# A hybrid encoder block in fp32: value projection with 512 columns for six of eight token tiles, and three re-ordered places

## The reference

```python
u = rmsnorm(h); proj = u @ w_in                  # 1024 x 4096
qa, ka, va, hq, hff, hfb, hi, hg = split(proj, 512 each)
y_na = neighbourhood_attention(qa, ka, va)       # 8 heads of 64, grid 16 x 64, window 8 x 16
y_hg = bidirectional_gated_recurrence(hq, hff, hfb, hi, hg)   # 4 heads of 128, v = hi
h = h + concat(y_na, y_hg) @ w_out
u = rmsnorm(h); h = h + square(relu(u @ w_up)) @ w_down       # hidden 4096
```

## Time and profile before

| | us |
|---|---|
| three runs | 1292.2, 1293.55, 1294.88 |
| median | 1293.55 |
| profiled execution | 1293.81 |
| its span, first to last instruction | 1292.0 |
| PE / weight loads / DVE / ACT / POOL busy | 1274.4 / 1072.9 / 845.6 / 587.4 / 473.9 |

### The profile page before, as it was taken

How to read it: one execution, slowest core, us unless ns; L and a number is a source line. 1 busy time by engine, 2 the same in 40 slices (tenths; PEclk the granted TensorE clock), 3 DMA queues, 4 the chain that set the end, 5 groups by cost and what they waited for, 6 DMA issues and landing times.

```text
span 1292.0 us, 17686 instructions
## 1 busy us (share of the span) xinstructions
PE 1274.4 (99%) x6432; PEld 1072.9 (83%) x6432; DVE 845.6 (65%) x1268; ACT 587.4 (45%) x1058; POOL 473.9 (37%) x259
## 2 busy tenths in 40 slices
PE   7999999999999999999999999999999999999998
PEld 6878888998888889878888788888888888888887
DVE  3537666641869686976486654554555888888885
ACT  6346766445536354350345554454453433433341
POOL 3241212115030503045135544444443544544452
PEclk9999999999999999999999999999999999999999
DMA  7341332222010202152311744544559463533423
GB/s 247 129 131 49 82 103 83 83 66 82 1 50 1 66 1 68 47 185 74 134 49 58 243 139 146 166 137 145 166 203 374 138 238 98 190 133 102 162 86 144
DMA packets 134469, 154.92 MB, mean 120 GB/s; under 512 B 11376, under 2 KB 89584, under 8 KB 134384
## 3 DMA queue, kind: packets, MB, share of 16 engines
q1 hardware_dynamic: 131216, 147.04, 35.7%
q10 hardware_dynamic: 3168, 6.75, 1.4%
HBM read 109.72 MB, written 44.04 MB: 119 GB/s over the span
## 4 chain that ended last, share of the span: by engine, by line
PE 92%; DVE 4%; ACT 1%; issue 1%; DMA 1%; POOL 0%; ACTq 0%; SPq 0%; DVEq 0%
PE bank L2359 8%; PE bank L2362 8%; PE bank L2363 8%; PE bank L2328 7%; PE bank L2331 7%; PE bank L2332 7%; PE bank L2070 6%; PE bank L2066 6%; PE bank L2069 6%; PE bank L2153 4%; PE bank L2289 2%; PE bank L2285 2%; PE bank L2288 2%; PE bank L1964 1%; PE bank L1966 1%
## 5 line engine op out<-in xcount | busy, mean ns | idle before, releaser
L885 POOL TENSOR_TENSOR w_hi<-stage,one_col 128x1024 fp32r<-128x1024 f32 x32 | 61.3, 1917 | 409.6 <-DVE scores L1615 176.4
L943 POOL TENSOR_TENSOR a_split<-a_raw,a_split 128x1024 fp32r<-128x1024 f32 x56 | 148.0, 2663 | 166.1 <-ACT a_split L1223 166.1
L2328 PE MATMUL bank<-set,w_hi 128*128 128x512 f32 x448 | 177.8, 397 | 0.7 <-DVE s L1860 0.6
L2331 PE MATMUL bank<-set,w_hi 128*128 128x512 f32 x448 | 176.1, 393 | 0.0
L2332 PE MATMUL bank<-set,w_lo 128*128 128x512 f32 x448 | 176.0, 393 | 0.0
L2359 PE MATMUL bank<-w_hi,a_split 128*128 128x512 f32 x448 | 174.6, 390 | 0.2
L2363 PE MATMUL bank<-w_hi,a_split 128*128 128x512 f32 x448 | 174.3, 389 | 0.0
L2362 PE MATMUL bank<-w_lo,a_split 128*128 128x512 f32 x448 | 174.3, 389 | 0.0
L2066 PE MATMUL bank<-uT_hi,w_hi 128*128 128x512 f32 x384 | 158.7, 413 | 0.0
L2070 PE MATMUL bank<-uT_hi,w_lo 128*128 128x512 f32 x384 | 150.5, 392 | 0.0
L2069 PE MATMUL bank<-uT_lo,w_hi 128*128 128x512 f32 x384 | 149.7, 390 | 0.0
(11 more groups left out here) (227 smaller groups left out, 2748.9 us busy)
## 6 DMA issues: line engine op xcount, KB each, us to landing
a_raw<-a_dram SPq DMA_DIRECT2D x56, 512.0 KB, 3.8
a_dram<-abuf SPq DMA_DIRECT2D x111, 256.0 KB, 2.1
stage<-in_w_in SPq DMA_DIRECT2D x29, 512.0 KB, 4.1
raw<-in_w_down SPq DMA_DIRECT2D x10, 1024.0 KB, 8.0
stage<-in_w_up SPq DMA_DIRECT2D x16, 512.0 KB, 5.1
raw_b<-in_w_up SPq DMA_DIRECT2D x16, 512.0 KB, 5.7
x_tok<-in_x SPq DMA_DIRECT2D x8, 512.0 KB, 8.5
v_dram<-vs ACTq DMA_DIRECT2D x16, 256.0 KB, 2.3
```

The lines of the kernel that those rows point to most:

```text
L943: pool.tensor_tensor(split_of(m, 1), a_raw[:, m % 4, :, :], split_of(m, 0).bitcast(F32), ALU.subtract).then_inc(b_lo, 1)
L2328: first = pe.matmul(dst, w[0], u[0], start=k == 0 and p in (1, 5, 6, 7), stop=False, skip_group_check=True)
L2331: pe.matmul(dst, w[0], u[1], start=False, stop=False, skip_group_check=True)
```

## The change

1. Value units. Token tiles 0 and 1 keep two units of 256 columns each; token tiles 2 to 7 get one unit of 512 columns, ("hv", 2, t), over all four value tiles. The order is ("hv", 0, 0), ("hv", 0, 1), the six wide units, ("hv", 1, 0), ("hv", 1, 1). A wide unit is cut into two pieces of four feature blocks. The sixteen pieces stand at the places of the sixteen units before. PE gives back two ring slots at the first matmul of ("hv", 1, 0), and two at the first after ("hv", 1, 1).
2. Tile 15 is split without the wait for the bias.
3. Tile 35 is split after `o_sq_rest >= 8` instead of after the last level; SP loads all residual tiles before tile 37.
4. In block 2 of the up products DVE makes `up_results` before the sums of weights of block 3.
5. The first query-key mean stands after four feature blocks of the next unit instead of two.

```diff
-    u += [("hv", c, t) for c in range(2) for t in range(TT)]
+    u += [("hv", 0, t) for t in HALF_TOKENS] + [("hv", 2, t) for t in FULL_TOKENS] + [("hv", 1, t) for t in HALF_TOKENS]
...
-VALUE_UNITS = {9: (0, 1), 10: (2, 3), 11: (4, 5, 6), 12: (7, 8, 9), 13: (10, 11), 14: (12, 13), 15: (14, 15)}
-VALUE_AT = {(s, 2 * i if s == 9 else i): j for s, js in VALUE_UNITS.items() for i, j in enumerate(js)}
+VALUE_PIECES = [(("hv", 0, t), range(KT)) for t in HALF_TOKENS]
+VALUE_PIECES += [(("hv", 2, t), ks) for t in FULL_TOKENS for ks in (range(4), range(4, KT))]
+VALUE_PIECES += [(("hv", 1, t), range(KT)) for t in HALF_TOKENS]
+VALUE_STEPS = {9: (0, 1), 10: (2, 3), 11: (4, 5, 6), 12: (7, 8, 9), 13: (10, 11), 14: (12, 13), 15: (14, 15)}
+VALUE_AT = {(s, 2 * i if s == 9 else i): j for s, js in VALUE_STEPS.items() for i, j in enumerate(js)}
...
-                if n == N_IN + RING + 2:
-
                     sp.wait_ge(o_mean, 2 * HG_HEADS)
                     load_resid(range(3, TT))
...
-                if 10 <= n < 16:
+                if 10 <= n < 15:
                     pool.wait_ge(bias_done, bias_ops(2 * n - 19))
...
+                elif n == N_IN + RING - 1:
+                    pool.wait_ge(o_sq_rest, 2 * HG_HEADS)
...
-                    act.activation(h_v[:, part, 256 * what:256 * what + 256], b[:, 0:256], ACT.Copy).then_inc(act_freed, 1)
+                    c0, w = (0, 512) if what == 2 else (256 * what, 256)
+                    act.activation(h_v[:, part, c0:c0 + w], b[:, 0:w], ACT.Copy).then_inc(act_freed, 1)
...
+                if j == 2:
+                    up_results(j)
                 if j == UPS - 1:
                     down_weights(0)
                 else:
                     for p in (7, 5):
                         up_sum(UP_AT[(j + 1, p)])
-                up_results(j)
+                if j > 2:
+                    up_results(j)
...
-                    done = 2 * (p1 == TT - 1)
+                    done = 2 * ((UNITS[n - 1][1], p1) in ((2, TT - 1), (1, HALF_TOKENS[-1])))
...
-                    tile = TILE_OF[("in", C_HV + 256 * what)]
-                    pe.wait_ge(w_split, 2 * (tile + 2))
+                    c0, tiles = (0, 4) if what == 2 else (256 * what, 2)
+                    tile = TILE_OF[("in", C_HV + c0)]
+                    pe.wait_ge(w_split, 2 * (tile + tiles))
...
-                        w = [t[:, r:r + 2, P * k:P * k + P] for t in ring]
-                        dst = b[:, 0:256]
+                        w = [t[:, r:r + tiles, P * k:P * k + P] for t in ring]
+                        dst = b[:, 0:P * tiles]
...
-                projection(n, range(2))
+                ahead = 4 if n == FIRST_QK + 1 else 2
+                projection(n, range(ahead))
                 qk_average(n - 1)
-                projection(n, range(2, KT))
+                projection(n, range(ahead, KT))
```

More of the change, by code:

```diff
@@ L128 @@
 N_TILES = len(TILES)
+HALF_TOKENS, FULL_TOKENS = (0, 1), tuple(range(2, TT))
 def proj_units():
@@ L995, in unit @@
                 elif kind == "hv":
-                    if what == 0 and part < NG:
+                    if what != 1 and part < NG:
                         act.wait_ge(score_done, NG * (NB * (PAIRS - 1) - 1) + part + 1)
-                    act.activation(h_v[:, part, 256 * what:256 * what + 256], b[:, 0:256], ACT.Copy).then_inc(act_freed, 1)
+                    c0, w = (0, 512) if what == 2 else (256 * what, 256)
+                    act.activation(h_v[:, part, c0:c0 + w], b[:, 0:w], ACT.Copy).then_inc(act_freed, 1)
                 elif kind == "hq":
@@ L1273, in _ @@
                     qk_root(qk)
-                values = [UNIT[("hv", 0, 0)] + i for i in VALUE_UNITS.get(s, ())]
-                for n in values[:1] if s > 9 else ():
+                values = [VALUE_PIECES[j] for j in VALUE_STEPS.get(s, ())]
+                values = [[UNIT[u]] if ks[-1] == KT - 1 else [] for u, ks in values] + 4 * [[]]
+                for n in values[0] if s > 9 else ():
                     unit(n)
@@ L1278, in _ @@
                     take_pT(s, 2)
-                for n in values[1:2] if s > 9 else ():
+                for n in values[1] if s > 9 else ():
                     unit(n)
@@ L1282, in _ @@
                     take_pT(s, 3)
-                for n in values[2:]:
+                for n in values[2]:
                     unit(n)
@@ L1295, in _ @@
                     if s == 9 and g == 1:
-                        unit(values[0])
+                        unit(values[0][0])
                 if s == 9:
-                    unit(values[1])
+                    unit(values[1][0])
                 if s >= 0:
@@ L2223, in share @@
                     if (s, i) in VALUE_AT:
-                        projection(UNIT[("hv", 0, 0)] + VALUE_AT[(s, i)])
+                        u, ks = VALUE_PIECES[VALUE_AT[(s, i)]]
+                        projection(UNIT[u], ks)
                 if s >= 0:
```

## The result

The changed kernel took 1299.57 us in the median of six runs (1298.39 to 1301.24); the kernel before, beside it on the same chip, 1293.04 (1292.2 to 1294.88). The ratio is 1.0046, with a 95% interval of 1.0036 to 1.0057: slower by about 6 us, a small loss but clear of the noise (the medians differ by 6.5). The profiled execution took 1300.29 us with a span of 1298.5, which is 6.5 more than the span of before.

A forecast was written before the change was run, and what follows sets the result against it. TensorE (PE), busy 99% of the span, was taken as the bound; gains of 4.8 us against costs of 10.55 gave net +5.7 on 1293.81, less 0.26: 1299.3 us, range 1295.0 to 1303.0.

The forecast's parts named there:

- the main step: At step 15, later slot return delays tile 16's split, tile 18's load and band 15 behind it; PE waits 8.05 us.
- T: Moment PE starts the first matmul of ("hv", 1, 0), the first piece of step 15; 281.98 in the kernel before.
- Stall: PE's wait for band 15 before step 15's first product with it: 8.05 us, bounds 7.7 and 9.3.
- POOL's part: POOL starts splitting tile 16 at T + 0.51 and has it split at T + 4.9.
- the landing: Time from issue to landing of band 15's last DMA, behind tile 18's load: taken as 2.4 us.
- Clock: PE's clock falls in the wait for band 15 and slows the rest of step 15: 2.0 us lost, bounds 0 and 3.
- rival 2: The wait for band 15 comes but PE's clock stays up: 1297.3 us; chance 15%.
- Step 9: Tile 15's earlier split on POOL meets DVE's two probability multiplies: cost 0.5 us, bounds 0 and 1.4.
- Values: Twelve value pieces with 512-column instead of 256-column matmuls save 1.3 us on PE, bounds nothing and 1.7.
- First mean: Six more matmuls before the first query-key mean cover its 0.9 us wait: gain 0.9, bounds 0.5 and 0.9.
- Late split: Tile 35's split waits for head 3's o_sq_lo pair, removing PE's 2.0 us wait before the second head mean; bounds 1.6 and 2.4.
- Up order: In the up block, DVE adding block 2's results first removes PE's wait: gain 0.6 us, bounds 0.4 and 0.7.

The follow-up runs named there:

- Experiment 1: Changed kernel with band 15's loads moved ahead of tile 18's in SP's program; 1288.29 us, ratio 0.9963 to the kernel before.
- experiment 4: Changed kernel with band 15's eight loads issued once PE gives back the slot, before the wait for tile 16's split; 1295.46 us, ratio 1.0008.
- Experiment 6: Changed kernel with band 15 ahead of tile 18 and all five query-key means before the attention steps behind four feature blocks; 1288.21 us.
- experiment 3: Kernel before with only the 512-column value units, tile 15's early split and band 15 ahead of tile 18; 1293.14 us, ratio 0.9996.

## Why the prediction was right, and where its terms were off

The forecast was 1299.3, the result 1299.57, and the main step came as described: T sets POOL, POOL sets tile 18, tile 18 stands in front of band 15, PE waits for its last DMA. Experiment 1 shows the cause by removing nothing but the order in the queue. But several terms were off, and partly for each other.

- **Stall: 9.01 instead of 8.05.** POOL's part was right (T + 4.83 for T + 4.9), as was the issue of the band (last one at T + 8.77 for T + 8.6). The term that was too small is the landing: 3.1 us after the issue, where I took 2.4. Both neighbours were in the earlier trace rows, 2.1 and 3.3; I put the higher one down to the store beside it, and with no store but a 512 KB tile load in front it was 3.1 too. In experiment 4, with POOL's split beside it but the tile load behind, the band's last DMA landed 2.05 us after its issue. The load in front is the part that counts.
- **Clock: 1.65 instead of 2.0.** It fell, as the slow start of the earlier trace rows let one expect; rival 2 is out. What spoke for it, a column that prints 1.00 throughout, was no evidence, since the clock's record begins after the slow start. The Trainium skill (TensorE: Matmul & The Clock Gate, "What's actually happening") has idling return the array to its lower rate; the granted clock of 0.50 behind the wait agrees. That 1.65 came near 2.0 is partly luck: experiment 4's shorter wait cost 2.44.
- **Step 9: 1.05 instead of 0.5.** The mechanism was named and bounded (0 to 1.4). The value taken between the ends was too low: POOL and DVE started within 0.01 us of each other, too close to say which was first, and DVE's pair took 4.57 us, near the 4.21 of the earlier trace rows.
- **Values: 0.95 instead of 1.3.** Added up over the stretch from step 10 to T, the distances from each value matmul to the next start fell from 35.42 us (288 matmuls) to 34.15 (144), so 1.27: the rate of 0.230 us of the earlier trace rows holds for these operands too (276.66 to 276.89 in one piece). The 0.3 that is missing is in the first products with 256 columns right behind a piece, five in the stretch: 0.66 us to the next start before, 0.97 after. What delays them was not followed further. The rule of the Trainium skill on warm matmuls (TensorE: Matmul & The Clock Gate, "Wait — 56ns, not 53.3ns?") would have given an estimate of 0.4; the rows of the trace gave the better price.
- **First mean: nothing instead of 0.9.** This is the step whose mechanism failed. The prediction said that the next mean "is 6 us away", and took that for enough. Those 6 us are the distance before (6.45); the six matmuls that go ahead of the first mean are taken out of it, 18 are left of 24, and the chain of ACT and DVE between two means takes 6.12 us. So PE, which no longer waits 0.93 at the first mean, waits 0.73 at the second, and the second starts 14.28 us after the first query unit where it was 14.35. Experiment 6 puts the 24 back and shows that the wait only moves on: ACT and DVE set the pace there, not the place of the mean.
- **Late split: 2.67 instead of 2.0.** The waits before both means are gone (L2218 below), and the two `o_sq_lo` take 1.29 us without POOL. All of the 2.67 lies there: from the first output product to the one behind the means PE took 572.92 - 566.44 = 6.48 us before and 580.19 - 576.39 = 3.80 now. The prediction counted only the longer of the two waits; the list's 2.2 holds both, and a wait costs more in distance than its idle time: the first mean started 0.59 us after the matmul ahead of it (569.68 - 569.09) for an idle time of 0.19, where 0.23 is usual.
- **Up order: 0.79 instead of 0.6**, which were the wait alone, as with the late split.

The last head in the changed kernel, DVE, and then PE at the two means, to be compared with the earlier trace rows:

```profile
577.82 1.29 DVE L1655 TENSOR_TENSOR o_sq_lo<-tmp,o_sq_hi 128x512 fp32r<-128x512 f32 x2 [0.98 <-ACT o_sq_hi L1145]
```

```profile
579.26 0.40 PE L2218 MATMUL bank<-o_sq_hi,mean_r 128*128 128x512 f32 x1
...
579.73 0.39 PE L2218 MATMUL bank<-o_sq_hi,mean_r 128*128 128x512 f32 x1
```

Gains were 0.95 + 2.67 + 0.79 = 4.4 where I had 4.8, costs 9.01 + 1.65 + 1.05 = 11.7 where I had 10.55. The sum is +7.3 for +5.7; the start-up, 0.83 earlier in this profile by chance, brings the span to +6.5. That the total lies within 0.3 us of the forecast is therefore partly luck: an error of 1.5 us in the sum was covered by the spread of the start-up and by the base, the median of the kernel before being 1293.04 in six runs where the forecast had 1293.55 from three.

## What to carry to other kernels

When slots of a ring are given back later, follow everything that stands behind the refilling load in the same queue, down to data that has nothing to do with the ring: here one list entry was worth 10.7 us (the stall and its clock). A wait that goes is a gain only if the chain that made it is shorter than the work until its next turn, so lay the length of the chain beside the distance that is left after the move. And where small terms are in question, measure distances between fixed points on the bounding engine; the totals here spread by 2 us and more within one kernel, and five of the seven terms are smaller.

## What the runs showed of the hardware

- The granted clock fell to 0.50 in waits of 8.85 and 3.81 us; after a wait of about 2.0 us it fell in the profile of experiment 3 (matmuls 0.43 us apart from 570.53 to 573.51, where 0.233 is usual there) and not in that of the kernel before. The shorter of the two long waits cost more in its profile, 2.44 against 1.65 us, because PE then worked longer until the clock was back: about 5.3 against 3.5 us.
- DVE operations on operands in SBUF lasted as long as POOL's split beside them: the pair of multiplies 4.57 us instead of 0.68, three bias operations 2.82 instead of 1.22, the pair of `o_sq_lo` 4.43 instead of 1.29. The Trainium skill (GPSIMD Engine Reference, "1. Specifications") has the two engines share their way to SBUF, with contention for DVE instructions that have two inputs in SBUF or run in a mode that uses two ports. The bias operations and `o_sq_lo` have two such inputs and agree with it; the multiplies have one tensor input, and in which mode they ran no run here shows.
- The last of eight 64 KB loads behind a 512 KB one landed 3.1 us after its issue (293.14 - 290.04), against a median of 2.1 in the earlier trace rows with nothing just ahead. Four such issues took 2.92 us at 281.75 in experiment 4, against 1.73 in the earlier trace rows; one of the four alone took 1.62.
- The record of the granted clock can begin late: in the kernel before it starts at 15.30 us, and the column prints 1.00 ahead of that while 512-column matmuls start 0.43 us apart.
